# A hybrid decoder trunk on one core: Silu in chunks behind the convolutions, normalisation factors later, sums of squares in four quarters

## The reference

```python
h = rms_norm(x, mix_norm[l])
(dq, dk, dv, iq, ik, iw, gq, gk, gv, gz, ga, gb, mq) = split_columns(h @ w_in[l])
# A: sparse attention, 6 heads of 64, queries and keys RMS-normed per head
qa = rms_norm(dq.reshape(B, T, 6, 64), dsa_q_norm[l])
ka = rms_norm(dk.reshape(B, T, 6, 64), dsa_k_norm[l])
out_a = dsa_attention(qa, ka, va, q_idx, ik, w_idx, rel_bias)
# B: gated DeltaNet, 6 heads of 64, chunks of 64 tokens
q, k, v = split(silu(causal_depthwise_conv(concat([gq, gk, gv]), conv_w)))
qh = l2_norm(q) * 64 ** -0.5;  kh = l2_norm(k)
o = gated_delta_rule_chunked(qh, kh, vh, g, beta)
out_b = rms_norm(o, out_gain) * silu(gz)
# C: attention into 256 memory tokens, 4 heads of 64
qh = rms_norm(mq, q_gain);  kh = rms_norm(km, k_gain)
x = x + concatenate([out_a, out_b, out_c]) @ w_out[l]
```

## Time and profile before

| | us |
|---|---|
| Median of 3 runs | 2143.65 |
| Lowest, highest run | 2141.34, 2144.3 |
| Profiled execution | 2149.74 |
| Its span in the profile | 2148.0 |
| Mean granted TensorE clock, share of full | 0.996 |

### The profile page before, as it was taken

One profiled execution on the slowest core, in us unless ns is written; L12 is line 12 of the kernel. 1 busy time (PEld: TensorE's weight loads), 2 busy tenths in 40 slices (PEclk: granted clock), 3 DMA queues, 4 the chain that ended last, 5 costly groups with the idle time before them and its releaser, 6 DMA issues.

```text
span 2148.0 us, 31599 instructions
## 1 busy us (share of the span) xinstructions
PE 2123.0 (99%) x13057; PEld 1717.3 (80%) x13057; DVE 1044.9 (49%) x1419; ACT 758.8 (35%) x1046; POOL 356.3 (17%) x293
## 2 busy tenths in 40 slices
PE   9999999999999999999999999999999999999999
PEld 7888888777777888888888888887777778888887
DVE  5343333688756543433333433337887655433322
ACT  5222222474435422222232222234744454222211
POOL 0111011105013411101111010111041135010000
PEclk9999999999999999999999999999999999999999
DMA  5222222221111232223222222232212102222232
GB/s 194 93 93 92 99 99 106 106 96 44 67 44 40 79 114 91 93 90 106 94 98 98 98 98 91 94 130 95 84 41 91 40 20 101 95 98 98 93 108 74
DMA packets 30643, 192.38 MB, mean 90 GB/s; under 512 B 3216, under 2 KB 5392, under 8 KB 11984
## 3 DMA queue, kind: packets, MB, share of 16 engines
q1 hardware_dynamic: 30160, 189.80, 25.2%
q10 hardware_dynamic: 384, 1.14, 0.1%
HBM read 188.70 MB, written 2.10 MB: 89 GB/s over the span
## 4 chain that ended last, share of the span: by engine, by line
PE 90%; DVE 6%; ACT 2%; issue 1%; DMA 0%; SPq 0%; POOL 0%; DVEq 0%; ACTq 0%
PE psum L895 27%; PE psum L897 26%; PE psum L896 26%; PE psum L1325 2%; PE psum L1026 1%; PE psum L1309 1%; PE psum L1198 1%; PE psum L1195 1%; PE psum L1293 1%; DVE acc L1831 1%; DVE wl L1748 1%; DVE XL L1763 1%; DVE gkT L1862 0%; DMA raw<-weights 0%; DVE cv L1894 0%
## 5 line engine op out<-in xcount | busy, mean ns | idle before, releaser
L895 PE MATMUL psum<-XH,wh 128*128 128x512 f32 x1904 | 762.2, 400 | 4.9 <-DVE wl L1748 1.8
L897 PE MATMUL psum<-XH,wl 128*128 128x512 f32 x1904 | 744.1, 391 | 0.0
L896 PE MATMUL psum<-XL,wh 128*128 128x512 f32 x1904 | 744.0, 391 | 0.0
L895 PEld LDWEIGHTS psum<-XH,wh 128*128 128x128 f32 x1904 | 358.7, 188 | 93.8 <-issue 14.7
L897 PEld LDWEIGHTS psum<-XH,wl 128*128 128x128 f32 x1904 | 358.8, 188 | 75.8
L896 PEld LDWEIGHTS psum<-XL,wh 128*128 128x128 f32 x1904 | 359.1, 189 | 74.4 <-issue 4.3
L1756 DVE TENSOR_TENSOR wl<-raw,wh 128x2048 fp32r<-128x2048 f32 x88 | 201.7, 2292 | 159.4 <-ACT wh L1395 159.4
L895 PE MATMUL psum<-HH,wh 128*128 128x512 f32 x704 | 273.9, 389 | 0.0
L896 PE MATMUL psum<-HL,wh 128*128 128x512 f32 x704 | 273.9, 389 | 0.0
L897 PE MATMUL psum<-HH,wl 128*128 128x512 f32 x704 | 273.9, 389 | 0.0
L1390 ACT ACTIVATE wh<-raw 128x2048 fp32r<-128x2048 f32 (+1 forms) x84 | 157.3, 1872 | 301.2 <-PE psum L897 301.2
(11 more groups left out here) (250 smaller groups left out, 1966.2 us busy)
## 6 DMA issues: line engine op xcount, KB each, us to landing
raw<-weights SPq DMA_DIRECT2D x143, 1024.0 KB, 4.8
raw<-weights SPq DMA_DIRECT2D x32, 896.0 KB, 4.4
xT<-xt SPq DMA_DIRECT2D x4, 512.0 KB, 6.9
memT<-memt SPq DMA_DIRECT2D x2, 1024.0 KB, 4.7
out<-xT SPq DMA_DIRECT2D x8, 256.0 KB, 6.0
stripsA<-strip_table SPq DMA_DIRECT2D x2, 768.0 KB, 6.7
raw<-weights SPq DMA_DIRECT2D x2, 512.0 KB, 7.0
stripsB<-strip_table SPq DMA_DIRECT2D x2, 512.0 KB, 7.5
```

Of the source, the lines that this page charges most:

```text
L895: pe.matmul(out_ap, a_hi, b_hi, start=first, stop=False)
L896: pe.matmul(out_ap, a_hi, b_lo, start=False, stop=False)
L897: return pe.matmul(out_ap, a_lo, b_hi, start=False, stop=last)
```

## The change

Silu becomes twelve steps of one chunk (512 columns). Chunks 0 to 2 (q) stand behind convolution 6, chunks 3 to 5 (k) behind 7, chunks 6 and 7 behind 8, chunk 8 in the first `gz` group, 9 in the second, 10 and 11 behind the third. The Silu table is loaded once ahead of chunk 0, the other table once behind chunk 11 (`exp_ln`): two loads in the place of four.

The sums of squares go in pairs throughout: for odd nj, four f32 matmuls of 64 rows by 64 columns take each half of both chunks. Chunk i's halves go to bank 2+i; those of the odd chunk are written crossed (upper half of the rows to the lower half of the bank), and Ln, now two instructions on 64 partitions each, uncrosses them. In the projections `hs` of pair 0 moves from ahead of the first `gz` eviction to behind the third `gz` group, `hs` of pairs 1, 2 and 3 behind `mk1`, `mv1` and the sixth of eight steps of `mq0`; the other steps follow. The first transposes now stand behind all of `mq0`. In the inversion a pair's `hs` follows the square of its odd chunk.

The diff, whole:

```diff
--- before.py
+++ after.py
@@ -231,7 +231,7 @@
     put("copy")
     early = [["smt"], ["mem3", "gate1"], ["gate3"], ["mem5"], [], ["gate4"], ["gate6"], [], []]
     late = [[], ["mem4", "gate2"], [("idx", 0)], [("idx", 1)], [], [("idx", 2), "gate5"], [("idx", 3), "gate7"],
-            ["silu_qk"], []]
+            [], []]
     for n in range(9):
         name, c = ("gq", "gk", "gv")[n // 3], n % 3
         mm(name, c)
@@ -239,45 +239,51 @@
         ev(name, c)
         put(("tap", n), ("conv", n))
         put(*late[n])
+        if n >= 6:
+            put(*(("silu", i) for i in range(3 * n - 18, min(3 * n - 15, 8))))
         if n == 7:
             norm("sq", *pairs(0))
 
     def factors(i):
-        for kind in ("hs", "rs", "ap"):
+        for kind in ("rs", "ap"):
             norm(kind, *pairs(i))
 
     mm("gz", 0)
-    factors(0)
     ev("gz", 0)
-    norm("sq", *pairs(1))
-    put(("idx", 4))
+    put(("silu", 8), ("idx", 4))
     sel(1)
     mm("gz", 1)
-    factors(1)
     ev("gz", 1)
-    norm("sq", *pairs(2))
-    put(("idx", 5))
+    put(("silu", 9), ("idx", 5))
     mm("gz", 2)
+    norm("hs", pairs(0)[1])
     ev("gz", 2)
-    put("silu_vz")
+    put(("silu", 10), ("silu", 11), "exp_ln")
+    factors(0)
+    norm("sq", *pairs(1))
     sel(2)
     mm("mk", 0)
     ev("mk", 0)
     mm("mk", 1)
+    norm("hs", pairs(1)[1])
     ev("mk", 1)
-    factors(2)
-    norm("sq", *pairs(3))
+    factors(1)
+    norm("sq", *pairs(2))
     sel(2)
     mm("mv", 0)
     ev("mv", 0)
     sel(2)
     mm("mv", 1)
+    norm("hs", pairs(2)[1])
+    ev("mv", 1)
+    factors(2)
+    norm("sq", *pairs(3))
+    sel(2)
+    order.append(("mm", GROUP_AT["mq", 0], 0, 6))
+    norm("hs", pairs(3)[1])
     factors(3)
-    ev("mv", 1)
-    sel(2)
-    order.append(("mm", GROUP_AT["mq", 0], 0, 4))
+    order.append(("mm", GROUP_AT["mq", 0], 6, KD))
     put(("vt", 0), ("vt", 1))
-    order.append(("mm", GROUP_AT["mq", 0], 4, KD))
     ev("mq", 0)
     sel(1)
     fill = []
@@ -286,7 +292,7 @@
         fill += [(name, c, k, 0.68) for k in range(KD)]
     fill += [("v", b, k, 0.5) for ks in (range(0, V_SPLIT), range(V_SPLIT, KD)) for b in range(2) for k in ks]
     fill += [("v", b, k, 0.5) for b in (2, 3) for k in range(KD)]
-    later = [(1, ("sq", 8)), (2, ("hs", 8)), (2, ("rs", 8)), (3, ("ap", 8))]
+    later = [(1, ("sq", 8))]
     debt = 0.0
 
     def pull(target):
@@ -312,7 +318,10 @@
                         later.extend([(0, ("hi", v, 0, KD)), (1, ("lo", v, 0, KD // 2)), (3, ("lo", v, KD // 2, KD))])
                 if (name, c) in NORMS:
                     nj = NORMS.index((name, c))
-                    later.extend([(0, ("sq", nj)), (2, ("hs", nj)), (2, ("rs", nj)), (3, ("ap", nj))])
+                    later.append((0, ("sq", nj)))
+                    if nj % 2:
+                        later.extend([(2, ("hs", nj)), (2, ("rs", nj - 1)), (3, ("rs", nj)),
+                                      (3, ("ap", nj - 1)), (4, ("ap", nj))])
 
     for i, step in enumerate(INVERSION):
         order.append(step)
@@ -1017,14 +1026,17 @@
                     def head_sums(nj):
                         n = NM if NORMS[nj][0] == "mk" else T
                         pe.wait_ge(S["nq_sq"], nj + 1)
-                        if nj == 0:
+                        if nj == 1:
                             pe.wait_ge(S["row_ready"], 1)
-                        if nj == 8:
+                        else:
+                            pe.wait_ge(S["nq_r"], nj - 1)
+                        if nj == 9:
                             pe.wait_ge(S["v_done"], NB)
-                        if nj >= 2:
-                            pe.wait_ge(S["nq_r"], nj - 1)
-                        pe.matmul(bank[2 + nj % 2][:, 0:n], const("same64"), nsq[nj % 2][:, 0:n],
-                                  start=True, stop=True).then_inc(S["nq_ss"], 1)
+                        for i in range(2):
+                            for par in range(2):
+                                mm = pe.matmul(bank[2 + i][rows[par ^ i], 0:n], const("ones")[rows[par], 0:DH],
+                                               nsq[i][rows[par], 0:n], start=True, stop=True)
+                            mm.then_inc(S["nq_ss"], 1)
 
                     def index_scores(batch):
                         b, h0 = 1 + batch // 2, 4 * (batch % 2)
@@ -1115,7 +1127,7 @@
                             wait_copied(N_GROUPS - 2)
 
                     def value_transposes(b):
-                        pe.wait_ge(S["silu_done"], 3)
+                        pe.wait_ge(S["silu_done"], 9)
                         if b == 0:
                             pe.wait_ge(S["nq_r"], 8)
                         if b >= 2:
@@ -1464,7 +1476,7 @@
                         if nj >= 2:
                             act.wait_ge(S["nq_done"], nj - 1)
                         if name in ("gq", "gk"):
-                            act.wait_ge(S["silu_done"], 2)
+                            act.wait_ge(S["silu_done"], nj + 1)
                         else:
                             wait_copied(GROUP_AT[name, c])
                         src = {"dq": dqT, "dk": dkT, "mq": mqT, "mk": mkT, "gq": gqT, "gk": gkT}[name][:, c, :]
@@ -1475,8 +1487,16 @@
                         name = NORMS[nj][0]
                         n = NM if name == "mk" else T
                         act.wait_ge(S["nq_ss"], nj + 1)
-                        rsqrt(nrr[nj % 2][:, 0:n], bank[2 + nj % 2][:, 0:n], 1.0 / DH if name in ("mk", "dk") else 1.0,
-                              const("eps64") if name in ("dq", "mq") else None).then_inc(S["nq_r"], 1)
+                        scale = 1.0 / DH if name in ("mk", "dk") else 1.0
+                        bias = const("eps64") if name in ("dq", "mq") else eps
+                        if nj % 2 == 0:
+                            rsqrt(nrr[nj % 2][:, 0:n], bank[2 + nj % 2][:, 0:n], scale, bias).then_inc(S["nq_r"], 1)
+                            return
+                        for par in range(2):
+                            chain.step(act.activation(nrr[1][rows[par], 0:n], bank[3][rows[1 - par], 0:n], ACT.Ln,
+                                                      bias=bias[rows[par], :], scale=scale))
+                        chain.join()
+                        act.activation(nrr[1][:, 0:n], nrr[1][:, 0:n], ACT.Exp, scale=-0.5).then_inc(S["nq_r"], 1)
 
                     def index_relu(batch):
                         w = P * (2 + batch // 2)
@@ -1536,16 +1556,17 @@
                         elif kind == "gate7":
                             act.wait_ge(S["row_ps"], 1)
                             act.activation(rowg[:, :], bank[2][0:H_B, :], ACT.Copy).then_inc(S["row_ready"], 1)
-                        elif kind in ("silu_qk", "silu_vz"):
-                            if kind == "silu_qk":
-                                act.wait_ge(S["conv_done"], 6)
-                            else:
-                                act.wait_ge(S["conv_done"], 9)
-                                wait_copied(GROUP_AT["gz", 2])
-                            for t in ((gqT, gkT) if kind == "silu_qk" else (gvT, gzT)):
-                                f = t.rearrange("p c t -> p (c t)")
-                                act.activation(f, f, ACT.Silu).then_inc(S["silu_done"], 1)
+                        elif kind == "exp_ln":
                             act.preload_act_table_set(EXP_LN)
+
+                    def silu(n):
+
+                        if n < 9:
+                            act.wait_ge(S["conv_done"], n + 1)
+                        else:
+                            wait_copied(GROUP_AT["gz", n - 9])
+                        t = (gqT, gkT, gvT, gzT)[n // 3][:, n % 3, :]
+                        act.activation(t, t, ACT.Silu).then_inc(S["silu_done"], 1)
 
                     def value_copy(b):
                         act.wait_ge(S["v_t"], b + 1)
@@ -1663,6 +1684,8 @@
                             index_relu(*at_)
                         elif kind == "tap":
                             tap(*at_)
+                        elif kind == "silu":
+                            silu(*at_)
                         elif kind == "vt":
                             value_copy(*at_)
                         elif kind == "att":
```

## The result

| | before | changed |
|---|---|---|
| Median beside each other, us | 2143.98 (6 runs) | 2151.87 (6 runs) |
| Lowest, highest run | 2141.34, 2149.28 | 2151.1, 2153.23 |
| Profiled execution, span | 2149.74, 2148.0 | 2151.1, 2149.3 |
| Its mean granted clock | 0.996 | 0.994 |

The ratio is 1.0025, 95% interval 1.0014 to 1.0037: slower, by 5.4 us (3.0 to 7.9). The medians of these six and six runs are 7.9 us apart. The prediction was 2143, with a range up to 2150.

A forecast was written before the change was run, and what follows sets the result against it. TensorE, busy 99% of the span, was taken as the bound. Terms of -5.0, -0.9, +4.0 and +1.7 gave -0.2 us a layer, -0.4 in all, so 2143 from a median of 2143.65, range 2136 to 2150.

The forecast's parts named there:

- the difference carries over to the median: Whole kernel: -0.4 us on the profiled 2149.7, which stood 6.1 above the median 2143.65, was applied to that median, giving 2143.2.
- C: Projections: new TensorE waits for squares, mk's eviction and norm 7 ahead of the transposes, 4.0 us a layer lost.
- D: Around transposes and six-row matmuls: one more 3.4 us stretch at half clock a layer, 1.7 us lost.
- the walk to pair 3: In mq0, from the end of mv1: TensorE arrives at 5.4 us, the square ends at 6.6, a wait of 1.2.
- A: Head sums in projections, inversion and recurrence: four overlapping quarters do a pair's work, 5.0 us a layer won.
- Rival R1: Head sums: quarters writing one bank take turns, 6.5 us a layer, 13 in all, 2156; chance 0.06.
- B: Ahead of the first pair of sums: its stall on ScalarE goes, 0.9 us a layer won.
- The table load: ScalarE: a load costs 1.28 us by the trace, without the further drain of some 1.38 us the skill page states.
- rival R2: Projections: the clock falls more often, three stretches a layer in place of one, +3.2 us a layer, 2150; chance 0.12.
- At nothing: Effects sized at zero: fewer table loads, chunked Silu passes, additional half Lns and a later tap of chunk 7.
- the tap of chunk 7: Ahead of gz1: it moves about a microsecond later, within 1.2 us of room, so costs nothing.
- the half Lns: ScalarE: eight additional a layer, at most 0.67 us each, covered by its free time; without cover, factors 0.6 late.

The follow-up runs named there:

- e4_fill: Changed kernel with useless full-width products filling TensorE's two long waits, ahead of the sums behind mk1 and in mq0; 2149.43 us, ratio 1.0016 to the kernel before.
- e1_sums: Kernel before with quartered sums at their old places in the projections and by pairs in the inversion, Silu and loads as before; 2142.09 us, ratio 0.9979.
- e7_inversion: Kernel before with quartered sums only for the four pairs of the inversion and the recurrence; 2141.99 us, ratio 0.9977.
- e5_hybrid: Kernel before with quartered sums throughout and Silu of q and k alone in six chunks, four loads a layer, factors at old places; 2138.43 us, ratio 0.9966.
- e10_vt_late: Kernel before with only the first transposes moved behind all of mq0, directly ahead of the six-row matmuls; 2146.13 us, ratio 0.9997.
- e12 to e15: Kernel before with a stall ahead of mk1, idle or filled with products; then both with sums moved directly behind it; 2155.7, 2154.56, 2152.88, 2154.1 us.
- e2_full: Changed kernel with two full 128 by 128 sums in place of the four quarters, at the same places; 2155.46 us, ratio 1.0042 to the kernel before.

## Why the prediction was wrong

The forecast was 2143.2 and the median 2151.9. The 8.7 us are in three places.

1. **The transfer to the median: 6.1 us.** The step that failed is "the difference carries over to the median". The profiled execution of before had five low-clock stretches, and the sum kept those in the difference as if every run had them. Its runs have some 3.3 by the estimate above, and the three that made the median of 2143.65 were among its shortest. The changed kernel's clock is 0.9935 on average in six runs, that of before 0.9974 in the runs beside the experiments. A profiled execution far above the median, with stretches at the lower clock in it, was a sign on the table: the three runs shown lay at 2141 to 2144, where runs have clocks of 0.998 to 1.000. Against the 95 runs (2146.8) the change costs 5.1 us, where the sum had it gain 0.4.
2. **Terms C and D: 1.8 us against the profiled execution** (1.4 slower, -0.4 forecast). Pair 1's wait was sized 1.8 and is 2.3, pair 3's was sized 1.2 and is 2.8; those for mk's eviction and ahead of the transposes were sized 1.0 together and are 0 in layer 0 and 0.5 in layer 1. That is 5.1 us in layer 0 and 5.65 in layer 1, where 4.0 stood. Even this is flattered by the clock: in e4_fill, at full clock, the eviction costs 0.52 and the transposes 0.96, and with the filled time counted the four waits come to some 6.7 us a layer. The step that failed in C is the walk to pair 3: it lets the multiplication start at the end of ScalarE's Exp and gives it 0.65 us. It leaves out that VectorE's queue holds the split of the weights (2.8 us) ahead of both multiplications, and that each of these takes 1.25 here. An estimate from the rows: ScalarE's two Exp end at 484.22 and 486.31; had the split not stood there, the second multiplication would have ended at 487.56 in place of 488.31, 0.75 earlier, and another 0.6 at its usual length. These two make 1.35 of the 1.6 that were missing.
3. The last 0.8 us is the changed kernel's median over its profiled execution.

The near agreement of the two profiled executions with the sum (+1.3 us of span against -0.4) is partly luck, since the waits of C cost more and term A gave more than was put down.

Point by point:

- **A, size: right.** A 512-wide pair is 0.86 in the inversion, as four quarters on the chain (the step is 0.86 at 542.40 us; before, a single sum took 1.05 there, 0.20 of it the switch to the full array), and 1.1 by its own length in the projections. There, as at 480.60 us, the next full product starts 1.01 behind it and takes 0.34 in place of 0.23, so a pair costs 1.12 where the sum put 1.27. The 3.4 us a layer stand in the landmarks. Rival R1 is out. The rule of the Trainium skill's page "TensorEngine Tiling (Array Packing)", section "Restrictions and Gotchas", that different row tiles cannot access one PSUM bank at the same time does not show here: both row halves of a chunk went into one bank, and four quarters took the time of one. **A, worth: half.** e1_sums gave 4.5 of 10 us, the rest went into waits that shorter matmuls and longer factors open. e7_inversion gave 4.9 by the inversion alone.
- **B: right.** No wait is left ahead of the first pair, which stands at 463.18 with no idle time.
- **The table load: right.** Load 1.28 us, with the next instruction 0.02 us behind it in the chain above. The further drain that the Trainium skill's page "ScalarE: Activation LUTs", section "What ACT_TABLE_LOAD costs", states does not show. That two loads fewer have no worth was not tried by itself; the fastest kernel here, e5_hybrid, keeps all four.
- **D: the size right for the profiled execution and too small over the runs, the reason wrong.** It said one more stretch a layer, because transposes, wait and six-row matmuls adjoin. The profile has two more in layer 0 and one in layer 1 ahead of the recurrence, and one fewer behind it, seven against five: in the profiled executions the count of one more a layer is right. Over all runs it is not: by the estimate above, 8.2 against 3.3, that is some 2.5 more a layer. That is next to rival R2 (three more a layer, 2150), which the prediction gave a chance of 0.12. The additional stretches are at the waits ahead of the sums, and e10_vt_late shows that nearness of the transposes alone costs nothing. e4_fill shows that the idle waits next to the sums take part: filled, the mean clock is up by 0.0036. The price of 1.7 us for a stretch is too high there, 0.6 to 0.7 each, since the next wait takes up the rest.
- **At nothing: right for the tap of chunk 7** (no idle time between 435 and 463 us). **Wrong in part for the half Lns**: the walks of C count those of norms 1 and 5, 0.69 us each on the chain of pair 1, but e1_sums shows that in the projections they open waits at the old places of the factors too. The prediction's condition, that a pair's factors come late by 0.6 where the cover is gone, is what happened there.

**Open.** Idle time next to the sums of squares is where the clock fell in the changed kernel, but e12 to e15 did not turn this into a rule: idle between full products never did it at the spot, idle ahead of sums did it in one of two layers and left the mean clocks equal. e2_full has it in one of two layers too, ahead of full-width sums, so it does not take the quarters. Why the changed kernel has a low clock in each of its runs, and not in some, is shown only as far as e4_fill goes. That GpSimd's work is what slows VectorE at pair 3 is read from their overlap in time; it was not tried by itself, and the split at 384.85 us shows that an overlap alone does not do it.

## What to carry to other kernels

When a step moves, write down for each engine of its loop what now stands ahead of it in that engine's queue, the engine that only passes the result on included: here a split of weights on VectorE and multiplications at twice their usual length made a wait of 1.2 us into 2.8. Quartered or otherwise shortened matmuls give their time only where TensorE does not at once wait for what another engine makes of the result, so put them in the stretch with slack (the inversion) first; that alone gave 4.9 us (e7_inversion). Leave the factors at their places: with quarters throughout and only the Silu of q and k in chunks ahead of them, the kernel took 2138.4 us. And before a profiled execution stands for the median, compare its mean clock with that of the other runs.
